# Weight remainders, sums of squares and residual additions moved from GpSimd to VectorE in a two-layer Conformer/DeltaNet trunk

## The reference

```
for l in range(DEPTH):                                   # DEPTH = 2
    h = swiglu_ffn(rms_norm(x, ffn1_norm_pre[l]), ffn1_w_in[l], ffn1_w_out[l])   # 1024 -> 2*2816 -> 1024
    x = x + 0.5 * rms_norm(h, ffn1_norm_post[l])
    h = rms_norm(x, mix_norm_pre[l]) @ mix_w_in[l]       # columns: q, k, v, z (4 heads x 128), a, b, conv 2 x 512
    o_gdn = gated_deltanet_group(h, ...)                 # 4-tap causal convolution, chunked delta rule
    o_cm = conformer_conv_group(h, ...)                  # GLU, 31-tap causal depthwise convolution, layer norm
    h = jnp.concatenate([o_gdn, o_cm], axis=-1) @ mix_w_out[l]
    x = x + rms_norm(h, mix_norm_post[l])
    h = swiglu_ffn(rms_norm(x, ffn2_norm_pre[l]), ffn2_w_in[l], ffn2_w_out[l])
    x = x + 0.5 * rms_norm(h, ffn2_norm_post[l])
    x = rms_norm(x, block_norm[l])
```

## Time and profile before

| what | value |
|---|---|
| runs, us | 2331.14, 2334.84, 2342.38 |
| span of the profiled execution, us | 2341.6 |
| PE busy | 2114.6 us, 90% |
| DVE busy | 1133.3 us, 48% |
| POOL busy | 974.1 us, 42% |
| ACT busy | 685.0 us, 29% |
| L379 `wl<-raw,wh` on POOL | 340 instructions, 806.5 us |
| L395 `xt<-xt,upd` on POOL | 48 instructions, 75.3 us |
| L389 `acc<-acc,sqr` on POOL | 42 instructions, 54.3 us |

### The profile page before, as it was taken

One profiled execution on the slowest core, in us unless ns is written; L12 is line 12 of the kernel. 1 busy time (PEld: TensorE's weight loads), 2 busy tenths in 40 slices (PEclk: granted clock), 3 DMA queues, 4 the chain that ended last, 5 costly groups with the idle time before them and its releaser, 6 DMA issues.

```text
span 2341.6 us, 27451 instructions
## 1 busy us (share of the span) xinstructions
PE 2114.6 (90%) x9872; PEld 1756.6 (75%) x9872; DVE 1133.3 (48%) x1383; ACT 685.0 (29%) x909; POOL 974.1 (42%) x481
## 2 busy tenths in 40 slices
PE   5999998995988899999689999989859789999995
PEld 4888886774887688888568888868639767888884
DVE  6544301899754554430264442048997527444103
ACT  3222223323224322222342222233232243222223
POOL 3544455433112544445534444554340145444454
PEclk8999999997799999999889999999978899999996
DMA  4333333222001233333213333323210022333331
GB/s 122 108 99 99 92 94 93 72 63 81 1 1 37 63 104 93 99 91 99 80 56 99 98 92 95 93 61 90 72 54 1 1 72 69 93 98 96 90 101 45
DMA packets 349954, 179.58 MB, mean 77 GB/s; under 512 B 8402, under 2 KB 348852, under 8 KB 349876
## 3 DMA queue, kind: packets, MB, share of 16 engines
q1 hardware_dynamic: 348218, 178.44, 26.3%
q10 hardware_dynamic: 1658, 0.16, 0.1%
HBM read 176.48 MB, written 2.10 MB: 76 GB/s over the span
## 4 chain that ended last, share of the span: by engine, by line
PE 72%; DVE 19%; issue 5%; POOL 2%; ACT 1%; DMA 0%; DVEq 0%; POOLq 0%; SPq 0%; ACTq 0%
PE res L481 22%; PE res L482 21%; PE res L483 21%; DVE u L1144 8%; DVE cacc L1222 3%; POOL xt L395 1%; PE pq L660 1%; DVE acc L1051 1%; PE res L679 1%; DVE diag_l L1030 1%; DVE pre L1208 1%; POOL wl L379 1%; PE res L636 1%; DVE Tm L1311 1%; PE pq L702 1%
## 5 line engine op out<-in xcount | busy, mean ns | idle before, releaser
L379 POOL TENSOR_TENSOR wl<-raw,wh 128x1024 fp32r<-128x1024 f32 (+1 forms) x340 | 806.5, 2374 | 1098.5 <-ACT wh L782 1098.4
L481 PE MATMUL res<-xh,wh 128*128 128x512 f32 x1792 | 707.8, 395 | 58.6 <-DVE xl L1041 40.8
L482 PE MATMUL res<-xl,wh 128*128 128x512 f32 x1792 | 702.5, 392 | 0.0
L483 PE MATMUL res<-xh,wl 128*128 128x512 f32 x1792 | 702.2, 392 | 0.0
L782 ACT ACTIVATE wh<-raw 128x1024 fp32r<-128x1024 f32 (+1 forms) x340 | 352.5, 1038 | 1023.1 <-PE res L483 1020.8
L481 PEld LDWEIGHTS res<-xh,wh 128*128 128x128 f32 x1792 | 339.9, 190 | 140.8 <-issue 39.9
L483 PEld LDWEIGHTS res<-xh,wl 128*128 128x128 f32 x1792 | 339.4, 189 | 72.0
L482 PEld LDWEIGHTS res<-xl,wh 128*128 128x128 f32 x1792 | 340.1, 190 | 70.0
L1036 DVE RECIPROCAL rcol<-rsq 128x4 f32<-128x4 f32 x12 | 2.1, 179 | 579.5 <-ACT rsq L790 579.5
L481 PE MATMUL res<-hh,wh 128*128 128x512 f32 x704 | 273.9, 389 | 0.0
L482 PE MATMUL res<-hl,wh 128*128 128x512 f32 x704 | 273.9, 389 | 0.0
(11 more groups left out here) (235 smaller groups left out, 1758.7 us busy)
## 6 DMA issues: line engine op xcount, KB each, us to landing
raw<-in_ffn_w_in SPq DMA_DIRECT2D x180, 512.0 KB, 3.8
raw<-in_ffn_w_out SPq DMA_DIRECT2D x64, 448.0 KB, 3.4
raw<-in_mix_w_in SPq DMA_DIRECT2D x48, 512.0 KB, 3.9
raw<-in_ffn_w_out SPq DMA_DIRECT2D x32, 512.0 KB, 3.6
raw<-in_mix_w_out SPq DMA_DIRECT2D x16, 512.0 KB, 3.6
xin<-in_x SPq DMA_DIRECT2D x4, 512.0 KB, 5.1
out_dram<-xin SPq DMA_DIRECT2D x4, 512.0 KB, 2.7
crows<-in_cm_dw_w ACTq DMA_DIRECT2D x1, 62.0 KB
```

The source lines that it names most:

```text
L379: pool.tensor_tensor(wl[:, slot, 0:nk, :], raw[:, slot, 0:nk, :], wh[:, slot, 0:nk, :].bitcast(F32), ALU.subtract).then_inc(lo_full, 1)
L481: pe.matmul(res[:, bank, :], wh[:, slot, j, :], hi, start=first, stop=False)
L482: pe.matmul(res[:, bank, :], wh[:, slot, j, :], lo, start=False, stop=False)
L483: return pe.matmul(res[:, bank, :], wl[:, slot, j, :], hi, start=False, stop=last)
```

## The change

Three helpers move from GpSimd's program to VectorE's: the remainder (`low`, now named `weight_low`), `y_sum`, and the residual addition, which now stands in `update` right behind the `upd` that it needs. GpSimd keeps its few multiplications of `Dm` and the sums `lacc` in the mixer. On VectorE each `weight_low` is placed behind an eviction or at the end of a unit's work. The core of the diff, with the part that it takes from GpSimd left out:

```diff
@@ -994 @@  VectorE
             st = Steps(dve, dve_step)
+            dve.sem_inc(lo_full, SLOTS)
...
+            def weight_low(n, slot, nk, l):
+
+                dve.wait_ge(hi_full, l * UNITS + n + 1)
+                dve.tensor_tensor(wl[:, slot, 0:nk, :], raw[:, slot, 0:nk, :],
+                                  wh[:, slot, 0:nk, :].bitcast(F32), ALU.subtract).then_inc(lo_full, 1)
+
+            def y_sum(m, stage, l):
+
+                if m > 0:
+                    n = stage * (KD - 1) + m
+                    dve.wait_ge(sq_ready, l * NSQ + ((2 * stage + 1) * KD + m + 1))
+                    if m > 1:
+                        dve.wait_ge(ysum, l * NYQ + (n - 1))
+                    dve.tensor_tensor(acc[:], acc[:], sqr[:, m % 2, :], ALU.add).then_inc(ysum, 1)
...
                 dve.tensor_tensor(upd[:, k % 2, :], yg[:, k, :], bc[:, :], ALU.mult).then_inc(upd_ready, 1)
+                dve.wait_ge(upd_ready, l * NXR + n + 1)
+                dve.tensor_tensor(xt[:, k, :], xt[:, k, :], upd[:, k % 2, :], ALU.add).then_inc(x_ready, 1)
...
                         dve.tensor_tensor(gs[:, q, :], res[:, 2 * q, :], rs[:], ALU.mult).then_inc(gate_scaled, 1)
+                        weight_low(n, 2 * q, sizes[2 * q], l)
...
                         dve.tensor_tensor(hl[:, i * 2 + q, :], hf[:], hh[:, i * 2 + q, :].bitcast(F32),
                                           ALU.subtract).then_inc(h_ready, 1)
+                        weight_low(n + 1, 2 * q + 1, sizes[2 * q + 1], l)
...
                 dve.wait_ge(h_ready, l * NP + (f + 1) * KF)
+                for m in range(KD):
+                    for v in range(3 * m + 4, 3 * m + 7):
+                        if v < 3 * KD:
+                            weight_low(u0 + IN_U + v, v % SLOTS, OUT_PARTS[v % 3][1], l)
+                        elif v < 3 * KD + 3:
+                            weight_low(u0 + IN_U + v, v % SLOTS, 8, l)
+                    y_sum(m, 2 * f, l)
                 row([1, 5][f], l, rcol)
+                weight_low(u0 + FFN_U + 3, 3, 8, l)
+
+            for n in range(SLOTS):
+                weight_low(n, n, 8, 0)
...
                             dve.tensor_tensor(ga[:], res[:, bank, :], rs[:], ALU.mult).then_inc(mix_free, 1)
+                            weight_low(MBASE + r + SLOTS, r % SLOTS, 8, l)
...
                             st.link(dve.tensor_tensor(glu[:, t, PADC:], ga[:], gb[:], ALU.mult))
+                            weight_low(MBASE + r + SLOTS, r % SLOTS, 8, l)
...
                                     ins.then_inc(cv_ready, 1)
+                        weight_low(MBASE + r + SLOTS, r % SLOTS, 8, l)
...
                         dve.wait_ge(mix_free, l * MIX_IN_U + r + 1)
+                        weight_low(MBASE + r + SLOTS, r % SLOTS, 8, l)
...
                 head_low(H - 1)
+                for m in range(KD):
+                    if m < KD - 1:
+                        weight_low(MBASE + MIX_IN_U + m + SLOTS, m % SLOTS, 8, l)
+                    y_sum(m, 1, l)
                 row(3, l, rcol)
+                weight_low(MBASE + MIX_U + 3, 3, 8, l)
```

More of the change, by code:

```diff
@@ L448, in _ @@
                         ins.then_inc(lsum, 1)
-                for m in range(KD):
-                    if m < KD - 1:
-                        low(MBASE + MIX_IN_U + m + SLOTS, m % SLOTS, 8, l)
-                    y_sum(m, 1, l)
-                low(MBASE + MIX_U + 3, 3, 8, l)
-                residual(1, l)
-                ffn(1)
-                residual(2, l)
         @block.tensor
@@ L1075, in ffn, with pairs @@
             def ffn(f, l):
+                u0 = UBASE[f]
                 row([0, 4][f], l, rcol)
-                with dve.Fori(0, KF // 2) as i:
+                def pairs(i, sizes):
                     dve.sem_clear(pair_step)
@@ L1081, in ffn @@
                     for q in range(2):
-                        n = i * 4 + (UBASE[f] + 2 * q + SLOTS)
+                        n = i * 4 + (u0 + 2 * q + SLOTS)
                         dve.wait_ge(unit_done, l * UNITS + n + 1)
                         dve.tensor_tensor(gs[:, q, :], res[:, 2 * q, :], rs[:], ALU.mult).then_inc(gate_scaled, 1)
+                        weight_low(n, 2 * q, sizes[2 * q], l)
                         dve.wait_ge(unit_done, l * UNITS + n + 2)
@@ L1092, in ffn @@
                                           ALU.subtract).then_inc(h_ready, 1)
+                        weight_low(n + 1, 2 * q + 1, sizes[2 * q + 1], l)
+                with dve.Fori(0, KF // 2 - 1) as i:
+                    pairs(i, [8, 8, 8, 8])
+                pairs(KF // 2 - 1, [OUT_PARTS[n % 3][1] for n in range(4)])
                 dve.wait_ge(h_ready, l * NP + (f + 1) * KF)
+                for m in range(KD):
[5 more added lines that the diff above has]
+                    y_sum(m, 2 * f, l)
                 row([1, 5][f], l, rcol)
+                weight_low(u0 + FFN_U + 3, 3, 8, l)
+            for n in range(SLOTS):
+                weight_low(n, n, 8, 0)
             with dve.Fori(0, L) as l:
```

38 lines of the change are left out of this document (removed).

## The result

The changed kernel takes 2284.19 us (median of 4 runs, 2278.87 to 2285.42), the kernel before on the same chip 2337.74 (4 runs, 2331.14 to 2342.38): a ratio of 0.976, 95% interval 0.974 to 0.979. The forecast was 2296 in a range of 2276 to 2316.

A forecast was written before the change was run, and what follows sets the result against it. TensorE bounds the FFNs, VectorE, blocked by GpSimd, the mixer's input product. Terms -33.0 - 2.5 - 2.4 + 1.5 - 2.0 = -38.4 us on the profiled 2341.6 give 2303.2, scaled by 0.9971 to 2296; range 2276 to 2316.

The forecast's parts named there:

- The input product: Mixer's input product, units 4 to 23: 39.7 us blocked time out, 23.0 of remainders in, 140.9 to 124.2 us per layer.
- Units 0 to 3 and the first passages: Stretch before each mixer's unit 4: blocking goes, four remainders come in, so unit 4 starts net 0.2 us later.
- the term of -33.0: Mixer's input product with the later start of unit 4: 16.5 us less per layer, 33.0 in both.
- The second passages: Passages before the two second FFNs: square sum, remainder, update loop and `diag_l` sum to -1.25 us each, -2.5 together.
- the square sums: Before each mixer and second FFN, VectorE takes over GpSimd's last square sum, 1.27 us, at 0.69: -0.6 each of four times.
- The start: Kernel start: four first remainders join VectorE's queue, yet first `xt` comes at 25.4 us in place of 27.45: -2.0.
- The layer ends: End of each layer: updates and residuals in one VectorE queue, +0.75 us each, +1.5 for both.
- The delta rule: Stage after the mixer's input product: keeps its GpSimd work and blocking, costed at nothing.
- Rival B: Delta rule: shorter TensorE idle time before it restores 2.4 GHz, 10 us a layer less: 2276; chance 0.09.
- A: Input product: half the gain, as VectorE also waits for half of ScalarE's 1.06 us rounding: 2317; chance 0.15.
- C: Input product: each remainder costs VectorE 2 us, so no change there, only the other terms: 2329; chance 0.06.
- D: Input product: moved remainders simply add to VectorE, 40 x 1.15 = 46 us with nothing back: 2375; chance 0.07.

## Why the prediction was right, and where it was off

**What bounds the kernel, and why the change pays.** Right, and shown by experiment. GpSimd's work cost VectorE its duration in the one stage where VectorE is the bound; giving GpSimd other work to read brings the loss back at 2.03 us a piece, and moving the product's remainders alone brings 19.4 us a layer. In the FFN, `hf` went from 2.20 to 0.69 us as forecast, and it bought nothing where TensorE is full. The total was hit less well than the mechanism: on the profile the sum was 2303.2 where 2276.8 was measured, 26.4 us apart, of which 14.7 are the delta rule and 11.7 the other terms below.

**The input product.** The forecast for each layer was 140.9 to 124.2; measured 121.5. Of the 2.7 us between them, 1.3 are blocked time that I had too low (41.0, not 39.7). The remainder was right: 1.14 us in place of 1.15 (1.222 in the profile, forecast 1.23). The rest is in the unit's joints: before, `cacc` to the next `pre` is 0.78 us from start to start; now `cacc` to `wl` is 0.66 and `wl` to `pre` 1.13, so that the 0.12 us that VectorE lost ahead of each of the 12 `pre` are gone, 1.4 us. TensorE did not wait for anything new there, as forecast. (The 276 remainders that the prediction puts outside the product are those of 1024 elements in the whole kernel; outside the product there are 340 - 48 = 292, which changes no term.)

**Units 0 to 3 and the first passages.** I had unit 4 starting 0.2 us later; it starts 1.4 and 1.1 us earlier, counted from the first passage's beginning. Three small terms were off. The four remainders cost 1.0 us there, not 1.4 (first `ga` to unit 4's: 8.98 us before, 9.98 after). The free `diag_l` gives 1.5, not 1.2. And the steps of the update loop, forecast at 2.7 us, take 2.59, as `upd` at 403.13 and 405.72 show, since a pair of `upd` and residual costs 1.33 us from start to start and not 1.4. With the product, the term of -33.0 measured -41.2 in the table's rows, into which, as they are cut, -31.8 of it falls (see below).

**The second passages, `diag_l`, the square sums.** -2.5 was forecast for the second passages and their row of the table has -2.0, but the two don't cover the same work. In the table a passage begins behind the last square sum (-0.6) and ends ahead of `diag_l` (-1.2); both terms fall into the rows of the FFNs and the output product. Cut like the table, the forecast was +1.1 for the second passages, measured -2.0; -3.6 for the first FFNs, measured -0.9; -3.6 for the second FFNs, measured -1.8; -1.2 for the output product, measured -3.5; +2.7 for the layer ends, measured +1.8. The near agreement of -2.5 and -2.0 is luck. The passages were better than forecast, in part by the shorter update loop above, in part by the small `col_h` ahead of it, which GpSimd had blocked (0.89 us at 776.51 before, 0.17 after). The FFNs were worse, for two reasons. TensorE's wait of 1.2 for `diag_l` went, but in each FFN a new one stands a little later, for `us` of the first unit (waits of TensorE, 25 to 420 us), and takes two thirds of it back:

```profile
PE res L427 <- DVE us L1053: 0.8, 1, 0.8
```

And the square sum's 0.6 buys nothing at the end of the first FFN, because ScalarE is the later one there: from its `sqr` to its `rsq` it takes 3.44 us in both kernels, without idle time ahead of `rsq`.

```profile
393.01 1.06 ACT L728 ACTIVATE wh<-raw 128x1024 fp32r<-128x1024 f32 x1
394.08 1.28 ACT L736 ACT_TABLE_LOAD   x1
395.38 0.26 ACT L736 ACTIVATE rsq<-stat,eps 128x4 f32<-128x4 f32 x1
```

At the end of the second FFN ScalarE had waited 0.42 us for it, and that much is gained.

**The start.** -2.0 forecast, -3.3 measured, with the start at 47.8 us; it is 47.5 to 49.0 in the kernels that have the same code there, so some of the 1.3 between them may be chance. The first `xt` comes at 24.41, not at 25.4. ScalarE's last `wh` ended at 22.33 and not at 22.93, and behind the remainder the small copies took 0.9 us where I had 1.3. The rows that answer to the earlier trace rows:

```profile
22.36 1.22 DVE L989 TENSOR_TENSOR wl<-raw,wh 128x1024 fp32r<-128x1024 f32 x1 [0.36 <-ACT wh L728]
...
24.41 1.41 DVE L1036 SCALAR_TENSOR_TENSOR xt<-xt,gblk,bc 128x512 f32<-128x512 f32 x2
```

**The layer ends.** The change loses there, as forecast: +1.8 measured, where the terms that fall into this row make +2.7 and the square sum ahead of it -1.2. In the kernel with GpSimd's additions back, 12.08 us of these again stand beside VectorE and block its `acc` (1.15 us in place of 0.69), and still the end is 0.76 us shorter: two queues of which each is slowed beat one here.

**The mixer's output product.** Of its -3.5 us the forecast has the square sums, 0.6 in each layer (TensorE's wait for `acc` went from 2.6 to 2.0 us). The other 2.3 are TensorE's clock again, not GpSimd. VectorE's four instructions `on` take 2.50 us together in both kernels, so nothing blocks them. What differs is the granted clock. Before, it is 1.00 in the 3 us ahead of the transposes, TensorE waits 2.5 us for `on`, and then it is 0.66 in the first 5 us of the stage. In the changed kernel it is 0.63 ahead, the wait is 1.0 us, and the clock is 1.00 behind it. Some kernels with the changed kernel's code there have one case in one layer and the other in the next: without the fills the stage is 48.12 us in the first layer, with 0.66, and 47.01 in the second, with 1.00. The transposes before, in the changed kernel, and without the fills:

```profile
728.28 1.73 PE L748 MATMUL pq<-ident,on 128*128 128x128 f32 x8 [2.46 <-DVE on L1377]
698.59 1.26 PE L694 MATMUL pq<-ident,on 128*128 128x128 f32 x8 [1.01 <-DVE on L1363]
695.56 1.97 PE L705 MATMUL pq<-ident,on 128*128 128x128 f32 x8 [2.44 <-DVE on L1374]
```

**The delta rule.** This is the step of the prediction that went wrong: "The delta rule keeps its GpSimd work and its blocking", with nothing for the clock. It measured -14.7 us in these two profiles, and some 3 to 7 at the medians by the estimate above. Rival B named the clock, with a chance of 0.09, and priced it at 10 us a layer. Its sign, a granted clock of 1.0 right behind the product, did not come: the first 10 us have 0.67 in the changed kernel as in the kernel before. Its condition, that TensorE's shorter idle time ahead is what brings the clock back, fell twice. The idle time shrank from 12.5 + 8.1 to 10.4 + 3.1 us in the changed kernel; in the run with the subtraction on GpSimd it is 14.4 + 6.7, longer than before, and the delta rules are 134.6 and 139.2 us all the same:

```profile
PE res L554 <- DVE Wm L1176: 14.4, 1, 14.4
PE stat L547 <- DVE gate_g L1159: 6.7, 1, 6.7
```

And in the run with unused matmuls TensorE was busy 10.00 of the 10 us ahead, and the dip came nevertheless. Nor was it all or nothing: behind the first 20 us some 16 us more at 1.2 GHz, or 7 to 10, or none came, by layer and execution.

**The scale.** I multiplied by 0.9971 because the profile was 0.3% above the median of three runs. That lowered the forecast by 7 us and partly made good for terms that were too small: my sum on the profile was 2303.2, and the changed kernel's profile had 2276.8.

**The rivals.** A is out: 0.6 us of waiting for `wh` in the product, where it wanted 10.6 a layer. C is out: 1.14 us and not 2. D is out for the change but exact for the doubled remainder, 1.15 us each. B is out as the cause that it named; that TensorE's clock moves the time by several us a layer is right.

## What to carry to other kernels

GpSimd's idle share is not free room. Look for the long ones among otherwise equal instructions on VectorE (2.89 against 0.75 us), put the excess beside the price of doing the work on VectorE itself (here 2.05 against 1.14 us), and move it where the excess is larger; only at the layer ends, where nothing else hides VectorE's queue, did two engines stay a little better than one. When a stage of many small matmuls has two lengths under the same code, look at its granted clock before explaining the difference, compare kernels that have the same code there, and take more than one profile.

## What was not expected of the hardware

- A GpSimd fill of 1024 elements (0.95 us) held one-input TENSOR_SCALARs of 512 elements up from 0.54 to 1.30 us, and left the two-input taps at 0.744.
- With unused matmuls ahead, TensorE's granted clock fell to 0.50 or 0.51 in the second 10 us of the delta rule in 3 of 4 layers (0.70 in the other), although it had been 0.96 to 1.00 in the 30 us before, after a window in which TensorE was busy 8.4 of 10 us, some 3.6 of them with 32 matmuls of one column. It came back within 10 us in these 3 (0.99 or 1.00 in the third window) and took 20 us more in the other (0.64 and 0.85), in one and the same execution as one of them.
- A longer wait of TensorE, 1.9 us in place of 0.8 at the FFN's start, was followed by some 4 us at a mean granted clock of 0.60, and cost 1.6 us on top of the wait.
